# Compressed attention scores in 16 products over both groups' queries, with block-wise keys

## What is computed

```python
def blk(i):                                        # of nsa_attention; B = 1, G = 2 groups, HPG = 4 heads in each, d = 64
    ...
    valid_c = cmp_end[None, :] <= tq[:, None]
    sc = jnp.einsum('bqghd,bngd->bghqn', qb, kc)   # kc: (B, 31, G, d), rotated
    pc = jax.nn.softmax(jnp.where(valid_c, sc, NEG), axis=-1) * valid_c
    o_c = jnp.einsum('bghqn,bngd->bqghd', pc, vc)
    ...
    return gb[..., 0:1] * o_c + gb[..., 1:2] * o_s + gb[..., 2:3] * o_w
```

## Time and profile before

| | us |
| --- | --- |
| median of 3 runs | 2059.97 (2059.74 to 2063.7) |
| the profiled execution | 2054.47 |
| its span, first to last instruction | 2052.8 |
| TensorE busy (matmul) | 1941.8 (95%) |
| VectorE busy | 1189.2 (58%) |
| ScalarE busy | 775.6 (38%) |
| GpSimd busy | 573.7 (28%) |
| mean granted TensorE clock | 0.971 of full |

### The profile page before, as it was taken

One profiled execution on the slowest core, in us unless ns is written; L12 is line 12 of the kernel. 1 busy time (PEld: TensorE's weight loads), 2 busy tenths in 40 slices (PEclk: granted clock), 3 DMA queues, 4 the chain that ended last, 5 costly groups with the idle time before them and its releaser, 6 DMA issues.

```text
span 2052.8 us, 25688 instructions
## 1 busy us (share of the span) xinstructions
PE 1941.8 (95%) x9708; PEld 1576.6 (77%) x9708; DVE 1189.2 (58%) x1998; ACT 775.6 (38%) x1314; POOL 573.7 (28%) x428
## 2 busy tenths in 40 slices
PE   7998889999999999998999999989999879999997
PEld 6885657888888888766888888878747777888876
DVE  4456576762464452285773376364448768766776
ACT  3245452432232143383332233254324264344342
POOL 2122350300000020182310001043240446766740
PEclk9999699999999999999999999999998989999999
DMA  6322002552353232203363255212110212333334
GB/s 218 111 87 83 1 1 102 193 201 100 116 191 123 82 103 102 84 2 103 114 205 133 96 178 202 82 62 71 59 76 1 103 62 102 118 108 123 123 134 153
DMA packets 38955, 221.16 MB, mean 108 GB/s; under 512 B 5888, under 2 KB 6336, under 8 KB 18368
## 3 DMA queue, kind: packets, MB, share of 16 engines
q1 hardware_dynamic: 27184, 177.89, 24.3%
q0 software_dynamic: 11664, 41.80, 6.3%
HBM read 215.55 MB, written 2.10 MB: 106 GB/s over the span
## 4 chain that ended last, share of the span: by engine, by line
PE 77%; DVE 14%; DMA 2%; POOL 2%; ACT 2%; issue 2%; SPq 0%; POOLq 0%; DVEq 0%; ACTq 0%
PE G L408 36%; PE G L2335 6%; PE G L2234 5%; PE TR L2335 4%; PE OB L2335 4%; PE G L1510 2%; PE G L2255 2%; PE TR L408 2%; POOL weights_low L431 1%; PE OB L408 1%; PE OB L1469 1%; PE OB L1510 1%; PE TR L1510 1%; PE TR L2234 1%; DMA KS_sb<-ada 1%
## 5 line engine op out<-in xcount | busy, mean ns | idle before, releaser
L408 PE MATMUL G<-xt_high,weights_high 128*128 128x512 f32 (+2 forms) x1288 | 476.6, 370 | 18.4 <-POOL xt_low L1226 5.8
L425 ACT ACTIVATE weights_high<-ring_sb 128x1024 fp32r<-128x1024 f32 (+1 forms) x312 | 321.7, 1037 | 416.3 <-PE OB L2335 134.2
L408 PE MATMUL G<-xt_high,weights_low 128*128 128x512 f32 (+2 forms) x1288 | 473.6, 368 | 0.0
L408 PE MATMUL G<-xt_low,weights_high 128*128 128x512 f32 (+2 forms) x1288 | 473.6, 368 | 0.0
L431 DVE TENSOR_TENSOR weights_low<-ring_sb,weights_high 128x1024 fp32r<-128x1024 f32 x204 | 250.6, 1233 | 383.6 <-ACT weights_high L425 375.4
L431 POOL TENSOR_TENSOR weights_low<-ring_sb,weights_high 128x1024 fp32r<-128x1024 f32 (+1 forms) x108 | 267.7, 2492 | 397.4 <-ACT weights_high L425 343.7
L408 PEld LDWEIGHTS G<-xt_high,weights_high 128*128 128x128 f32 (+1 forms) x1288 | 242.6, 188 | 60.9 <-issue 17.3
L408 PEld LDWEIGHTS G<-xt_high,weights_low 128*128 128x128 f32 (+1 forms) x1288 | 242.5, 188 | 40.1
L408 PEld LDWEIGHTS G<-xt_low,weights_high 128*128 128x128 f32 (+1 forms) x1288 | 242.7, 188 | 39.5
L2120 POOL DMA_DIRECT2D KS_sb<-ada x64 | 33.8, 529 | 477.0 <-DVE og_sb L2679 477.0
L1969 DVE SCALAR_TENSOR_TENSOR KS_sb<-G,cols_sb,KS_sb 128x441 f32<-128x441 f32 (+2 forms) x176 | 121.0, 687 | 73.6 <-ACT KS_sb L1725 73.6
(11 more groups left out here) (470 smaller groups left out, 3615.4 us busy)
## 6 DMA issues: line engine op xcount, KB each, us to landing
ring_sb<-chunks SPq DMA_DIRECT2D x156, 1024.0 KB, 4.8
KS_sb<-ada POOLq DMA_DIRECT2D x64, 512.0 KB, 4.8
ring_sb<-slabs SPq DMA_DIRECT2D x3, 2048.0 KB, 7.5
X_sb<-x SPq DMA_DIRECT2D x4, 512.0 KB, 6.6
rows_sb<-ln_gain POOLq DMA_DIRECT2D x4, 512.0 KB, 5.1
rows_sb<-ln_bias POOLq DMA_DIRECT2D x4, 512.0 KB, 5.9
out<-X_sb SPq DMA_DIRECT2D x4, 512.0 KB, 5.0
table_sb<-table SPq DMA_DIRECT2D x1, 1146.0 KB, 15.9
```

Source lines behind the costliest of these rows:

```text
L408: mm = nc.tensor.matmul(out, lhsT=a, rhs=b, start=(3 * i + j == 0), stop=(3 * i + j == n - 1))
L425: nc.scalar.activation(Wh[:, n % 4, c], raw_quarter(Q)[:, c], ACT.Copy).then_inc(w_hi, 1)
```

## The change

The two batches are cut by query tile, no longer by group. Batch x takes the query tiles 2x and 2x + 1. A product takes all 128 partitions of a query tile, both groups' heads, against all 62 columns of the rotated keys. For the result to keep the groups apart the keys are made block-wise: `kcc[:, 1, :]` is zeroed, and the rotation's last addition writes group 0's 31 keys on partitions 0 to 63 and group 1's on partitions 64 to 127, each into its own columns. A batch is 8 products in place of 16, and the two together 16 in place of 32. The bank holds 64 columns for each of 2 x 4 pairs of query and token tile.

On VectorE there are a memset more (in `keys_values`, before its wait), one addition more in `key_rope`, and each `masked` is two instructions, one for each group, since `PC` keeps its layout. The second batch waits for both instructions of `masked(0)`. The counts in `SMALL` follow.

```diff
-    SMALL = dict(lam=2, windows=5, gelu_in=20, gelu=22, kraw=25, krope=28, scmp=32, pcmp=37, fabs=39, fox=44)
+    SMALL = dict(lam=2, windows=5, gelu_in=20, gelu=22, kraw=26, krope=30, scmp=36, pcmp=41, fabs=43, fox=48)
...
-            def cmp_scores(g):
-                pe.wait_ge(s_small, SMALL["krope"] + g)
-                r = slice(g * HD, (g + 1) * HD)
-                for i in range(4):
+            def cmp_scores(x):
+                pe.wait_ge(s_small, SMALL["krope"] + 2 * x)
+                for i in range(2):
                     for t in range(TT):
-                        c = i * P + t * 32
-                        mm = nc.tensor.matmul(CB[:, c:c + N_CMP], lhsT=QT[r, 4 + i, t * P:(t + 1) * P],
-                                              rhs=kcc[r, 1, g * N_CMP:(g + 1) * N_CMP], start=True, stop=True)
+                        c = i * 256 + t * HD
+                        mm = nc.tensor.matmul(CB[:, c:c + 2 * N_CMP], lhsT=QT[:, 4 + 2 * x + i, t * P:(t + 1) * P],
+                                              rhs=kcc[:, 1, :], start=True, stop=True)
                 mm.then_inc(s_smallp, 1)
...
             def keys_values():
+                step(nc.vector.memset(kcc[:, 1, :], 0.0), wait=False)
                 dve.wait_ge(s_smallp, 2)
...
                 step(nc.vector.tensor_tensor(out=b_[:, 0:62], in0=CB[:, P:P + 62], in1=tab("cmp_sin"), op=ALU.mult))
-                step(nc.vector.tensor_tensor(out=kcc[:, 1, :], in0=a_[:, 0:62], in1=b_[:, 0:62], op=ALU.add), wait=False)
+                for g in range(2):
+                    r, c = slice(g * HD, (g + 1) * HD), slice(g * N_CMP, (g + 1) * N_CMP)
+                    step(nc.vector.tensor_tensor(out=kcc[r, 1, c], in0=a_[r, c], in1=b_[r, c], op=ALU.add), wait=False)
                 mark("krope")
 
-            def masked(g):
-                dve.wait_ge(s_smallp, 4 + g)
-                step(nc.vector.tensor_tensor(out=PC[:, :, :, g, 0:N_CMP], in0=CB[:, :].rearrange("p (i t n) -> p i t n", i=4, t=TT)[:, :, :, 0:N_CMP],
-                                             in1=mkt.unsqueeze(1).to_broadcast([P, 4, TT, N_CMP]), op=ALU.add), wait=g == 1)
+            def masked(x):
+                dve.wait_ge(s_smallp, 4 + x)
+                ps = CB[:, :].rearrange("p (i t c) -> p i t c", i=2, t=TT)
+                for g in range(2):
+                    step(nc.vector.tensor_tensor(out=PC[:, 2 * x:2 * x + 2, :, g, 0:N_CMP], in0=ps[:, :, :, g * N_CMP:(g + 1) * N_CMP],
+                                                 in1=mkt.unsqueeze(1).to_broadcast([P, 2, TT, N_CMP]), op=ALU.add), wait=x + g == 2)
```

## The result

| | before | changed |
|---|---|---|
| median, us | 2059.85 (4 runs) | 2045.49 (4 runs) |
| profiled execution, us | 2054.47 | 2043.46 |
| its span, us | 2052.8 | 2041.8 |

The ratio is 0.9935, 95% interval 0.9923 to 0.9947: faster by 14.4 us by the medians, by 11.0 by the two profiled executions. The forecast was 9.0 us less than before and 2051.0; the median is 0.5 us under the lower end of the range.

What follows compares the result with a forecast made beforehand. TensorE's chain was taken as the bound, passing to VectorE before L869. L869 9.2 us earlier, less 0.2 for its half clock, gave 9.0 us: 2059.97 - 9.0 = 2051.0 us, range 2046.0 to 2057.5.

Steps and rivals of the forecast that it cites:

- The products: TensorE's two compressed-score batches: 16 records each, 0.113 us apart at full clock, 1.8 us a batch.
- VectorE in front of L853: The added memset (0.1 us) and second rope addition (0.2 us) make TensorE start L853 0.3 us later.
- The clock: TensorE's clock stays full to the second batch's end, chance 0.55; rival: falls anyway at about 206.8, gain 5.5 us, chance 0.25.
- The path from L853 to L869: Chain through both batches, turns, scores and VectorE's steps: L853 starts at 202.0, L869 at 218.2, a gain of 9.2 us.
- the wait in front of the second batch: TensorE waits 0.1 us until both halves of the first masking are done and the bank may be overwritten.
- The masking's split: Each VectorE masking becomes two instructions, adding 0.15 us, or 0.15 to 0.2 for the second, before L869.
- the piece from L997 to L869: VectorE's path behind the second batch: 6.68 us in the old trace, forecast 6.85 with the longer masking.
- The idle before it: TensorE idles some 4 us before L869, ended by VectorE's means, where it idled 1.3; this probably brings the clock down.
- a longer L869: The clock falling in the idle before L869 costs 0 to 0.5 us there; 0.2 taken.
- late next: VectorE's 6.85 us behind L997 becomes late, while TensorE has only about 2.7 us of work at full clock.
- What the attention gains, the end gains: Behind the stretch TensorE has hardly any slack, so the attention's gain reaches the end if no transfer is late.
- before's half-clock spells fall elsewhere in each execution: Supposed reason why before's profiled execution was 5.5 us faster than the median, some 1.6 us for one L869.

Runs made afterwards that it cites:

- wide32: Changed kernel with every product issued twice, so 32 records of 128 rows by 62 columns per batch; 2050.78 us, ratio 0.9963 to before.
- narrow16: Kernel before with two of the four query tiles per batch, so 16 records of 64 rows by 31 columns; 2044.88 us, ratio 0.9935 to before.
- vector_only: Kernel before, its products unchanged, with the changed kernel's memset, two rope additions and split maskings; one execution, 2058.83 us.
- least_late: Changed kernel with VectorE's second masking, minimum and subtraction moved behind the means that L869 waits for; 2043.01 us, ratio 0.9931 to before.
- pad16: Changed kernel plus 16 unread one-column products behind the keys' swap product, restoring before's TensorE program length; 2054.47 us, ratio 0.9989 to before.
- before_again: Kernel before, run once more without edit; 2059.93 us against 2057.64 for before beside it, ratio 1.0015.

## Why the prediction was right, and where not

**The products.** Right: 16 records in each batch, 1.73 and 1.89 us on the chain against forecasts of 1.8, 0.110 us apart in wide32 against 0.113. **VectorE in front of L853.** Right, 0.3 us. **The clock.** Right in what decides, and it is the larger part: 6.5 of the 10 us up to L869. My reason was half right. I had argued from what stands in front of the fall, 2.7 us of narrow records alone, and from fewer and fuller records after the change. The runs show that the fewer records alone are enough (narrow16), that fuller ones are enough too if full in both directions (wide32), and not in one alone. None of the rows of before could tell this.

**The path from L853 to L869.** I had 16.2 us (202.0 to 218.2); it is 15.67. Three terms were too large. The wait in front of the second batch, 0.1, does not appear: the masking's two halves start at 206.69 us and are done when VectorE takes its next step at 207.33, and the turns last until the batch starts at 207.47. The masking's split costs 0.07, not 0.15 to 0.2 (vector_only). And the piece from L997 to L869, which holds that split, is 6.53 us, not 6.85 and not even before's 6.68: I had carried before's duration over, in which the last copy waited for turns that ran at half clock (it starts 2.31 us behind L997; now both copies follow VectorE's steps without a gap). A stretch copied from the old trace keeps a wait that the change removes.

**L869 itself.** The idle before it is 3.87 us, forecast about 4; the clock falls in it, as said. I took 0.2 us for a longer L869; it took 3.73 against 3.97, 0.2 less. Up to L2234 the attention gives 111.05 - 100.56 = 10.5 us less the 0.3 in front of L853: 10.2 where I had 9.0; of the 1.2 us between, 0.5 lie in front of L869 and 0.6 in it and behind it. Of the "late next" list VectorE's means are the one that came true; GpSimd's scaling and ScalarE's exponentials showed only once least_late had taken the means away.

**The rest of the program.** "What the attention gains, the end gains" held to 0.1 us in the profiled pair: from L2234 to the end it is 1740.1 and 1740.0 us. By the medians the end gained 12.0 to 14.4 us, 1.8 to 4.2 more than the attention's 10.2, and the sum has no term for that. The later landing in the first MLP, 1.1 us, goes with the program's length (pad16) and points that way, but in the profiled pair it is made up before the end, so I can't add it to the sum. Two sets of runs of one kernel differed by 2.3 us (before_again), which covers the 1.8; of the 14.4 about 2 us stay open, and no run explains them. Against the profiled execution the sum gave 2045.5 and the trace 2043.46.

**The scatter.** I had supposed that before's half-clock spells fall elsewhere in each execution and so make the scatter. In this stretch they don't: the clock falls 5.1 and 5.3 us behind L853, L2234 comes 111.05 and 111.02 us behind it, and the mean clock is the same in two executions 8.2 us apart. That the gain could be read from one trace and set against the median rests on this, and I had not known it.

**The range** was too short at its low end by 0.5 us for the first set of runs and just long enough for the second. Its 5 us under the forecast were taken from how far before's profiled execution lay under the median, which is scatter of before and no term of the sum. That they nearly covered the attention's 1.2 us and the unexplained rest is luck.

## What to carry to other kernels

In these traces a product of two float32 operands with weights of 128 columns and few columns beside them is paid by the record, 0.11 to 0.12 us at full clock, whether it has 1, 31 or 62 columns and 64 or 128 rows: merge such products over rows and columns, at the price of zeros in the operand. Read the granted clock behind each run of such records; here it made nearly twice as much as the halving (6.5 against 3.6 us), in work that the edit did not touch. When a duration is carried over from the old trace, look whether a wait stands in it that the edit takes away.

## What I had not expected of the hardware

Sixteen products of one column, 3.78 us, put TensorE at 1.2 GHz for 10.2 us and made the kernel 8 to 9 us longer, about 1 of it perhaps by the later landing. Six kinds of batch give two outcomes for the clock that neither rows, columns nor number explains alone. And sixteen short products more or less on one engine moved the wait for a load some 170 us later by 1.1 us, in all thirteen traces.
